# Two-block transformer stack on one core: the attention's score parts issued ahead of the rounds of transposes

## The chip, the cores and the metric

The kernel runs on one core of a Trainium2 chip, as one launch. The metric is the device time of a whole execution in microseconds (us), and the number compared is the median over runs. In this text PE is TensorE (matmuls and transposes), DVE is VectorE, ACT is ScalarE, POOL is GpSimd and SP is SyncE. Each engine works through its own queue in order, and engines wait for each other through semaphores.

## What is computed

Two blocks of two layers each, over 512 latent tokens and 256 context tokens of width 1024, in float32. Every layer is an attention mixer followed by a gated feed-forward net with a short convolution. The change touches only the attention of the first three layers. There the reference is, cut to the core:

```python
def diff_attn(q, k, v, lam):          # layers 0 and 1: 4 heads, 2 maps each
    s = jnp.einsum("bqhmd,bkhmd->bhmqk", q, k) * (B_QK_DIM ** -0.5)
    p = jax.nn.softmax(s, axis=-1)
    a = p[:, :, 0] - lam * p[:, :, 1]
    return jnp.einsum("bhqk,bkhd->bqhd", a, v)

# layer 2: 8 heads of dense attention, 8 heads of attention to a
# neighbourhood (a bias masks the rest), heads taken in pairs
s = jnp.einsum('bgrqd,bgkd->bgrqk', q, k) * scale   # + bias
p = jax.nn.softmax(s, axis=-1)
o = jnp.einsum('bgrqk,bgkd->bgrqd', p, v)
```

Latent queries attend to 768 keys (512 latent, 256 context), context queries to the 256 context keys.

## The kernel before

**Steps.** `Attention` (with `paired_groups`) cuts the attention of a layer into groups and steps. A group is one head (layers 0 and 1) or one pair of heads (layer 2). A step is 128 queries of a group and always has two sides, e = 0 and e = 1: the two maps of a head, or the two heads of a pair. I call a step LAT0 to LAT3 for the four latent query tiles (768 keys) and CTX0, CTX1 for the two context tiles (256 keys). Layer 0 has 4 groups of six steps, layer 1 has 4 groups of LAT0 to LAT3 only, and layer 2 has 8 groups of six: four "plain" ones and then four "near" ones, whose latent steps carry the bias.

**What happens to a step n.** PE multiplies the scores of both sides into PSUM (`scores`, in parts of 512 and 256 keys for a latent step: S0 and S1 below; one part for a context step). DVE takes the row maxima (`maxima`, L1986; in a near step L1977 to L1983), ACT the exponentials (`exps`, L1465; near L1461 and L1462), DVE the reciprocals of the row sums (`reciprocals`, L1946 or L1948), POOL multiplies the probabilities by them (L693), and in layers 0 and 1 DVE subtracts the second map (`difference`, L1959). Some steps later PE transposes the probabilities in rounds of three or four 128x128 blocks (`turn`, L1013: rounds T0, T1, T2) into a single PSUM half bank, `TURNS`, and ACT (L1446) or DVE (L1925) copies each round out to `PTR`. Last, PE multiplies by the values (`values`, called V below).

**Software pipeline.** In step n PE issues the scores of step n and the transposes of step n - lag, where lag is 3 in layers 0 and 1 and 2 in layer 2. A latent step of layers 0 and 1 has two rounds, a latent step of layer 2 three (four blocks each; T1 holds the last two of side 0 and the first two of side 1), and a context step one round. In layers 0 and 1 ACT copies all rounds. In layer 2 DVE copies T0 and ACT copies T1 and T2.

**Queues.** There is no scheduler: each engine's order is the order of its own Python loop over n. What matters here:
- PE, before: T0, S0, T1, S1, V, T2, V.
- ACT: the output copy (if one is due), the copies of the rounds, and then the exponentials of step n.
- DVE: in layer 2 the copy of T0, then the low half of an output (L1934, after ACT's L1434) if one is due, then the reciprocals of step n-1, then the maxima of step n; in layers 0 and 1 the difference of step n-1 ends the list.
- POOL: the two multiplications (one in layers 0 and 1) of each step, once the reciprocals are there.

**Waits.** The scores lie in three PSUM banks that rotate over the sides. So the first part of side 0 waits until the exponentials of step n-2 are done, and the first part of side 1 until side 0 of step n-1 is:

```python
for e, (qt, kt, rows) in enumerate(G["maps"]):
    if a == 0 and A.side(n, e) >= 3:
        pe.wait_ge(S.exp_done, A.side(n, e) - 2)
```

A round of transposes waits for its probabilities (`p_ready`) and for the copy of the round before (`pt_ready` for ACT's copies, `pt_dve` for DVE's). DVE may begin the maxima when the last score part is done (`s_done`).

Of the kernel before, what the change touches and what calls it, by code (L numbers as in the profile page):

```python
# [101 lines left out]
def build(nc, d, out):  # L102
# [55 lines left out]
    with ctx:  # L158
# [420 lines left out]
        def scores_psum(A, n, e):  # L579

            return PS[(2 * n + e) % 3]
# [200 lines left out]
        def _(pe):  # L782
# [4 lines left out]
            def mm(o, a, b, start, stop):  # L787
                return pe.matmul(o, a, b, start=start, stop=stop)  # L788
# [86 lines left out]
            def rs_read():  # L875

                if w.taken.get(S.rs_free, 0):
                    pe.wait_ge(S.rs_free, w.taken[S.rs_free])
# [122 lines left out]
            def attention(A):  # L1001
                base = A.base

                def turn(r, n):

                    p_at = A.p_base + (n + 1 if A.diff else 2 * n + max(e for e, _ in r["chunks"]) + 1)
                    pe.wait_ge(S.p_ready, p_at)
                    if r["act0"]:
                        pe.wait_ge(S.pt_ready, r["act0"])
                    if r["dve0"]:  # L1010
                        pe.wait_ge(S.pt_dve, r["dve0"])
                    for k, (e, j) in enumerate(r["chunks"]):
                        last = pe.transpose(TURNS[:, k * P:(k + 1) * P], A.slot(n, e)[1][:, j * P:(j + 1) * P], IDENT)  # L1013
                    last.then_inc(S.t_done, 1)

                def scores(n, a, m, last):

                    G, u = A.steps[n]
# [3 lines that stand above are left out]
                        k0 = G["j0"] * P + a  # L1022
                        at = G["q0"] + u * P
                        step = mm(scores_psum(A, n, e)[:, a:a + m], qt[rows, at:at + P], kt[rows, k0:k0 + m], True, True)
                        if last:
                            step.then_inc(S.s_done, 1)

                def values(it):

                    G, u, j = it["G"], it["u"], it["j"]  # L1030
                    if j == 0:
                        act_n, dve_n = A.copied[it["step"]]
                        pe.wait_ge(S.pt_ready, act_n)
                        if dve_n:
                            pe.wait_ge(S.pt_dve, dve_n)
                    if it["opens"] and outs[0]:
                        pe.wait_ge(S.o_free, outs[0])
                    if it["opens"]:
                        outs[0] += 1
                    at, c0 = 256 * (it["half"] % 2), P * (u - 1)  # L1040
                    for e, rows in enumerate(G["rows"]):
                        last = mm(OUTS[rows, c0:c0 + 256], G["v"][e](G["j0"] + j), PTR[:, NTC * e + j, at:at + 256],
                                  j == 0, j == G["nj"] - 1)
                    if j == G["nj"] - 1:
                        last.then_inc(S.v_done, 1)

                rs_read()
                for n in range(A.n):
                    turns, items = A.turns(n), list(A.items[n])
                    parts = []  # L1050
                    if n < len(A.steps):
                        nk = A.steps[n][0]["nj"] * P
                        parts = [(a, min(512, nk - a)) for a in range(0, nk, 512)]
                    for k in range(max(len(turns), len(parts))):
                        if k < len(turns):
                            turn(turns[k], n - A.lag)
                        if k < len(parts):
                            scores(n, *parts[k], k == len(parts) - 1)
                        if k and items:
                            values(items.pop(0))  # L1060
                    for it in items:
                        values(it)
                act_n, dve_n = A.copied[-1]
                pe.wait_ge(S.exp_done, A.side(len(A.steps), 0))
                pe.wait_ge(S.pt_ready, act_n)
                if dve_n:
                    pe.wait_ge(S.pt_dve, dve_n)
                pe.wait_ge(S.o_free, base["outs"] + len(A.groups))
                w.taken[S.exp_done] = A.side(len(A.steps), 0)
                w.taken[S.pt_ready] = act_n  # L1070
                w.taken[S.o_free] = outs[0]
                w.taken[S.p_ready] = A.p_base + len(A.steps) * (1 if A.diff else 2)
# [14 lines left out]
            for li, L in enumerate(layers):  # L1087
# [42 lines left out]
                if blk == 0:  # L1130
# [24 lines left out]
                    rope(range(4, 12))  # L1155
                    pe.wait_ge(S.qk_ready, w.seen(S.qk_ready))
                    attention(L["attention"])
                    norm([(c,) for c in range(4, 8)], T, False, big)
                elif l == 0:
# [6 lines left out]
                    pe.wait_ge(S.qk_ready, w.seen(S.qk_ready))  # L1166
                    pe.wait_ge(S.swap_landed, 32)
                    attention(L["attention"])
                else:
                    linear(L["w_in"], HH, HL, None, S.h_ready)  # L1170
# [1268 lines left out]
```

## Time and profile before

| | us |
|---|---|
| runs shown, median (lowest to highest) | 4388.65 (4376.14 to 4388.95) |
| the profiled execution: device time | 4390.87 |
| its span | 4389.3 |
| attention of layer 0, 403.79 to 511 | 107.2 |
| attention of layer 1, 1530 to 1620 | 90.0 |
| attention of layer 2, 2342.89 to 2585 | 242.1 |

| share of the stretch in which the engine is busy | PE | DVE | ACT | POOL | granted clock |
|---|---|---|---|---|---|
| whole span | 89% | 44% | 28% | 8% | 0.91 |
| layer 0 attention | 89% | 59% | 53% | 40% | 0.81 |
| layer 1 attention | 89% | 58% | 52% | 39% | 0.82 |
| layer 2 attention | 85% | 54% | 54% | 72% | 0.95 |

The granted clock is TensorE's, as a share of full speed. The modelled end of a matmul includes its pipeline, and waits inside a group of merged rows count as busy, so the PE share reads high. Outside the three stretches nothing of the attention loop runs.

### The profile page before, as it was taken

To read this page: it belongs to the slowest core of one execution; us is meant where nothing else is said; L and a number is where in the kernel's file an instruction comes from. 1 tells how busy PE (TensorE), PEld (TensorE's weight loads), DVE (VectorE), ACT (ScalarE), POOL (GpSimd) and SP (SyncE) were. 2 spreads that over 40 slices of the span, in tenths; PEclk is the share of its full clock that TensorE was granted. 3 is DMA by queue.
4 is the path that set the end of the run, shared out by engine and by line. 5 is a ranking of instruction groups with operands and counts; after the bars stand their busy time and mean duration, and the time that the engine had idled before them with its cause. 6 is when DMAs were issued, how large, how long until landed. Compare 5 with 4: busy or idle time off the path is not lost.

```text
span 4389.3 us, 50022 instructions
## 1 busy us (share of the span) xinstructions
PE 3890.7 (89%) x20239; PEld 2987.2 (68%) x20239; DVE 1945.1 (44%) x2991; ACT 1236.5 (28%) x1931; POOL 344.1 (8%) x323
## 2 busy tenths in 40 slices
PE   6977889999989788999898886999996799978997
PEld 4865668888868556777784465888885445556775
DVE  3444554324355355434314546433435344445454
ACT  3222422112122142222223542211212344433221
POOL 1030300000000030000004740000000000000000
PEclk8976889999999579999998998999998789899998
DMA  4530013333322003545220101333321000012331
GB/s 169 156 84 1 1 58 111 96 92 113 89 63 72 1 1 102 156 137 160 72 58 13 26 28 51 116 95 93 115 82 38 23 16 16 23 49 68 91 96 63
DMA packets 500133, 317.33 MB, mean 72 GB/s; under 512 B 26832, under 2 KB 492526, under 8 KB 499904
## 3 DMA queue, kind: packets, MB, share of 16 engines
q1 hardware_dynamic: 492144, 299.80, 23.2%
q0 software_dynamic: 7760, 14.32, 1.2%
q8 instruction: 162, 2.65, 0.3%
q14 instruction: 67, 0.55, 0.0%
HBM read 309.61 MB, written 4.55 MB: 72 GB/s over the span
## 4 chain that ended last, share of the span: by engine, by line
PE 78%; DVE 12%; ACT 4%; issue 3%; POOL 2%; DMA 0%; DVEq 0%; ACTq 0%; POOLq 0%
PE PS L788 75%; PE PS L1013 1%; DVE TMP L1805 1%; POOL TMP L693 1%; DVE TMP L2380 1%; ACT SPH L1276 1%; DVE SPL L1724 1%; DVE HL L1788 1%; DVE TMP L1741 1%; PE PS L971 1%; DVE TMP L1797 1%; DVE X L1748 1%; DVE ATT L1986 1%; POOL BIG L693 1%; DVE X L2341 1%
## 5 line engine op out<-in xcount | busy, mean ns | idle before, releaser
L788 PE MATMUL PS<-HH,SPH 128*128 128x512 f32 (+1 forms) x3424 | 1240.7, 362 | 115.6 <-DVE HL L1788 69.1
L788 PE MATMUL PS<-HL,SPH 128*128 128x512 f32 (+1 forms) x3424 | 1217.2, 356 | 0.0
L788 PE MATMUL PS<-HH,SPL 128*128 128x512 f32 (+1 forms) x3424 | 1216.6, 355 | 0.0
L788 PEld LDWEIGHTS PS<-HH,SPH 128*128 128x128 f32 x3424 | 656.1, 192 | 258.7 <-issue 132.4
L788 PEld LDWEIGHTS PS<-HH,SPL 128*128 128x128 f32 x3424 | 655.3, 191 | 93.1
L788 PEld LDWEIGHTS PS<-HL,SPH 128*128 128x128 f32 x3424 | 657.2, 192 | 87.9
L1724 DVE TENSOR_TENSOR SPL<-RAW,SPH 128x1024 fp32r<-128x1024 f32 (+3 forms) x371 | 459.3, 1238 | 550.5 <-ACT SPH L1276 550.4
L1276 ACT ACTIVATE SPH<-RAW 128x1024 fp32r<-128x1024 f32 (+3 forms) x371 | 393.6, 1061 | 590.7 <-PE PS L788 483.0
L788 PE MATMUL PS<-MH,SPH 128*128 128x512 f32 (+1 forms) x1056 | 379.4, 359 | 18.1 <-DVE ML L2393 18.1
L788 PE MATMUL PS<-ML,SPH 128*128 128x512 f32 (+1 forms) x1056 | 377.3, 357 | 0.0
L788 PE MATMUL PS<-MH,SPL 128*128 128x512 f32 (+1 forms) x1056 | 377.2, 357 | 0.0
L2034 DVE SCALAR_TENSOR_TENSOR X<-PS,MOD,X 128x512 f32<-128x512 f32 (+1 forms) x144 | 95.3, 662 | 534.1 <-PE PS L788 532.3
L1681 ACT ACTIVATE TMP<-TMP 128x768 f32<-128x768 f32 (+1 forms) x88 | 65.0, 739 | 688.8 <-DVE TMP L2380 688.8
L788 PEld LDWEIGHTS PS<-MH,SPH 128*128 128x128 f32 x1056 | 202.0, 191 | 50.2 <-DVE ML L2393 21.8
L2371 DVE TENSOR_SCALAR TMP<-PS,PCOL 128x768 f32<-128x768 f32 (+1 forms) x88 | 83.0, 943 | 313.7 <-PE PS L788 303.7
L788 PEld LDWEIGHTS PS<-ML,SPH 128*128 128x128 f32 x1056 | 202.3, 192 | 28.3
L788 PEld LDWEIGHTS PS<-MH,SPL 128*128 128x128 f32 x1056 | 201.8, 191 | 28.7
L788 PE MATMUL PS<-BIG 64*128 64x256 f32 (+1 forms) x528 | 168.8, 582 | 17.5 <-issue 6.5
L2380 DVE SCALAR_TENSOR_TENSOR TMP<-PS,PCOL,TMP 128x511 f32<-128x511 f32 (+1 forms) x264 | 174.5, 661 | 21.9 <-DVE TMP L2380 0.5
L1686 ACT ACTIVATE MH<-TMP 128x768 fp32r<-128x768 f32 (+1 forms) x88 | 65.0, 738 | 322.9 <-DVE TMP L2387 322.9
L788 PE MATMUL PS<-ONES,TMP 128*128 128x1 f32 x276 | 57.6, 336 | 97.8 <-DVE TMP L1741 72.8
L1986 DVE TENSOR_REDUCE ATT<-PS 128x1 f32<-128x768 f32 (+1 forms) x144 | 105.2, 772 | 71.1 <-PE PS L788 71.0
(297 smaller groups left out, 4166.8 us busy)
## 6 DMA issues: line engine op xcount, KB each, us to landing
MS<-in_l_w_ada SPq DMA_DIRECT2D x96, 512.0 KB, 3.7
RAW<-in_l_w_up SPq DMA_DIRECT2D x88, 512.0 KB, 4.7
MS<-in_w_mod SPq DMA_DIRECT2D x80, 512.0 KB, 3.7
RAW<-in_w_gate SPq DMA_DIRECT2D x44, 512.0 KB, 4.9
RAW<-in_w_val SPq DMA_DIRECT2D x44, 512.0 KB, 4.9
RAW<-in_w_down SPq DMA_DIRECT2D x32, 704.0 KB, 4.7
RAW<-in_l_w_down SPq DMA_DIRECT2D x32, 704.0 KB, 4.6
RAW<-in_w_in SPq DMA_DIRECT2D x40, 512.0 KB, 5.3
```

The costliest lines, as they stand in the source:

```text
L693: pool.tensor_scalar(ex[:, 0:nk], ex[:, 0:nk], ATT[:, 3, k:k + 1], None, ALU.mult)\
L788: return pe.matmul(o, a, b, start=start, stop=stop)
L971: last = pe.transpose(STAT[:, j * P:(j + 1) * P], src[:, j * P:(j + 1) * P], IDENT)
L1013: last = pe.transpose(TURNS[:, k * P:(k + 1) * P], A.slot(n, e)[1][:, j * P:(j + 1) * P], IDENT)
L1276: act.activation(SPH[slot][:, 0:kc, 0:m], RAW[slot][:, 0:kc, 0:m], ACT.Copy).then_inc(S.hi_ready, 1)
L1681: act.activation(TMP[0][:, 0:T], TMP[0][:, 0:T], ACT.Silu)\
L1686: act.activation(MH[:, f, 0:T], TMP[1][:, 0:T], ACT.Copy)\
L1724: dve.tensor_tensor(SPL[slot][:, 0:kc, 0:m], RAW[slot][:, 0:kc, 0:m], SPH[slot][:, 0:kc, 0:m].bitcast(F32), ALU.subtract).then_inc(S.lo_re ...
L1986: dve.tensor_reduce(ATT[:, 0, k:k + 1], ps[:, 0:nk], AX.X, ALU.max, negate=True)\
L2034: dve.scalar_tensor_tensor(out=xc, in0=LIN[s % 2][:, a:a + k], scalar=g, in1=xc, op0=ALU.mult, op1=ALU.add)\
L2371: dve.tensor_scalar(g[:, 0:T], ps[:, 0:T], tap(1), par(li, "fb", f + f0), ALU.mult, ALU.add)\
L2380: dve.scalar_tensor_tensor(out=g[:, a + da:a + da + m - 1], in0=ps[:, a + sa:a + sa + m - 1], scalar=tap(k), in1=g[:, a + da:a + da + m - ...
```

## The change

In PE's loop over the steps the two calls inside the loop over k change places. The score part k now goes ahead of the round of transposes k. The queues of DVE, ACT, POOL and SP are word for word the same, and no wait is added or taken out.

```diff
                     for k in range(max(len(turns), len(parts))):
+                        if k < len(parts):
+                            scores(n, *parts[k], k == len(parts) - 1)
                         if k < len(turns):
                             turn(turns[k], n - A.lag)
-                        if k < len(parts):
-                            scores(n, *parts[k], k == len(parts) - 1)
                         if k and items:
                             values(items.pop(0))
```

PE in layer 2, a latent step whose three rounds are due (LAT2 of the first plain group). L788 with BIG or TMP_69 on the right are the scores of the two sides, L1013 the transposes. Before:

```order
L1013 MATMUL PS<-CST,TMP_67 128x128 [waits pt_ready,p_ready]
L1013 MATMUL PS<-CST,TMP_67 128x128 x3
L788 MATMUL PS<-BIG 128x512 [waits exp_done]
L788 MATMUL PS<-TMP_69,BIG 128x512 [waits exp_done]
L1013 MATMUL PS<-CST,TMP_67 128x128 [waits pt_dve,pt_ready,p_ready]
L1013 MATMUL PS<-CST,TMP_67 128x128
L1013 MATMUL PS<-CST,TMP_68 128x128 x2
L788 MATMUL PS<-BIG 128x256
L788 MATMUL PS<-TMP_69,BIG 128x256
L1013 MATMUL PS<-CST,TMP_68 128x128 [waits pt_dve,pt_ready,p_ready]
```

and now:

```order
L788 MATMUL PS<-BIG 128x512 [waits exp_done]
L788 MATMUL PS<-TMP_69,BIG 128x512 [waits exp_done]
L1013 MATMUL PS<-CST,TMP_67 128x128 [waits pt_ready,p_ready]
L1013 MATMUL PS<-CST,TMP_67 128x128 x3
L788 MATMUL PS<-BIG 128x256
L788 MATMUL PS<-TMP_69,BIG 128x256
L1013 MATMUL PS<-CST,TMP_67 128x128 [waits pt_dve,pt_ready,p_ready]
L1013 MATMUL PS<-CST,TMP_67 128x128
L1013 MATMUL PS<-CST,TMP_68 128x128 x2
L1013 MATMUL PS<-CST,TMP_68 128x128 [waits pt_dve,pt_ready,p_ready]
```

T0 moved behind S0, and with it behind the wait for `exp_done`; T1 moved behind S1.

DVE in layer 2, three latent steps in a row (the same in both kernels). L1925 copies T0, L1934 writes an output's low half, L1946 is the reciprocals of the step before, L1986 the maxima:

```order
L1925 COPY PTR<-PS 128x4x128 [waits v_done,t_done]
L1934 TENSOR_TENSOR HL<-PS,HH 128x512 [waits o_hi]
L1946 RECIPROCAL ATT<-ATT 128x2 [waits exp_done]
L1986 TENSOR_REDUCE ATT<-PS 128x1 [waits s_done] x2
L1925 COPY PTR<-PS 128x4x128 [waits v_done,t_done]
L1934 TENSOR_TENSOR HL<-PS,HH 128x256 [waits o_hi]
L1946 RECIPROCAL ATT<-ATT 128x2 [waits exp_done]
L1986 TENSOR_REDUCE ATT<-PS 128x1 [waits s_done] x2
L1925 COPY PTR<-PS 128x4x128 [waits v_done,t_done]
```

Nothing moved here: the copy of T0 stands ahead of the reciprocals and the maxima.

PE in layer 1, a latent step with its two rounds (BIG alone under L788 are the scores of both sides, VT the values). Before:

```order
L1013 MATMUL PS<-CST,TMP_67 128x128 [waits pt_ready,p_ready]
L1013 MATMUL PS<-CST,TMP_67 128x128 x2
L788 MATMUL PS<-BIG 128x512 [waits exp_done] x2
L1013 MATMUL PS<-CST,TMP_67 128x128 [waits pt_ready,p_ready]
L1013 MATMUL PS<-CST,TMP_67 128x128 x2
L788 MATMUL PS<-BIG 128x256 x2
L788 MATMUL PS<-PTR,VT 128x256 [waits pt_ready]
```

and now:

```order
L788 MATMUL PS<-BIG 128x512 [waits exp_done] x2
L1013 MATMUL PS<-CST,TMP_67 128x128 [waits pt_ready,p_ready]
L1013 MATMUL PS<-CST,TMP_67 128x128 x2
L788 MATMUL PS<-BIG 128x256 x2
L1013 MATMUL PS<-CST,TMP_67 128x128 [waits pt_ready,p_ready]
L1013 MATMUL PS<-CST,TMP_67 128x128 x2
L788 MATMUL PS<-PTR,VT 128x256 [waits pt_ready]
```

The last score part moved ahead of T1, whose wait for ACT's copy of T0 it no longer stands behind; T0 moved in between the two parts.

## Rows read from the trace of the kernel before

**Rows 1.** Timeline, layer 1: start us, us, engine line op out<-in xcount [idle before <-releaser].

```profile
1555.28 1.82 DVE L1986 TENSOR_REDUCE ATT<-PS 128x1 f32<-128x768 f32 x2 [2.81 <-PE PS L788]
...
1561.47 1.82 DVE L1986 TENSOR_REDUCE ATT<-PS 128x1 f32<-128x768 f32 x2 [2.81 <-PE PS L788]
...
1600.76 0.90 ACT L1465 ACTIVATE BIG<-PS,ATT 128x768 f32<-128x768 f32 x1 [1.19 <-DVE ATT L1986]
...
1601.43 1.50 PE L788 MATMUL PS<-BIG 64*128 64x512 f32 x4
...
1603.16 0.52 PE L1013 MATMUL PS<-CST,BIG 128*128 128x128 f32 x3 [0.23 <-ACT PTR L1446]
1603.61 0.70 PE L788 MATMUL PS<-BIG 64*128 64x256 f32 x4
...
1604.34 1.82 DVE L1986 TENSOR_REDUCE ATT<-PS 128x1 f32<-128x768 f32 x2 [1.26 <-PE PS L788]
1605.39 0.90 ACT L1465 ACTIVATE BIG<-PS,ATT 128x768 f32<-128x768 f32 x1 [1.19 <-DVE ATT L1986]
...
1608.97 1.82 DVE L1986 TENSOR_REDUCE ATT<-PS 128x1 f32<-128x768 f32 x2 [1.26 <-PE PS L788]
```

**Rows 2.** Timeline, layer 0: the maxima of LAT0 to LAT3 and the next LAT0.

```profile
435.70 1.82 DVE L1986 TENSOR_REDUCE ATT<-PS 128x1 f32<-128x768 f32 x2 [3.48 <-PE PS L788]
438.99 1.81 DVE L1986 TENSOR_REDUCE ATT<-PS 128x1 f32<-128x768 f32 x2
442.59 1.82 DVE L1986 TENSOR_REDUCE ATT<-PS 128x1 f32<-128x768 f32 x2
447.70 1.82 DVE L1986 TENSOR_REDUCE ATT<-PS 128x1 f32<-128x768 f32 x2 [1.64 <-PE PS L788]
...
459.87 1.82 DVE L1986 TENSOR_REDUCE ATT<-PS 128x1 f32<-128x768 f32 x2 [3.20 <-PE PS L788]
```

**Rows 3.** Timeline, layer 2, ACT: side 0's exponentials of one plain group, LAT0 to LAT0.

```profile
2401.26 0.90 ACT L1465 ACTIVATE TMP<-PS,ATT 128x768 f32<-128x768 f32 x1 [2.63 <-DVE ATT L1986]
...
2404.78 0.90 ACT L1465 ACTIVATE BIG<-PS,ATT 128x768 f32<-128x768 f32 x1 [1.65 <-DVE ATT L1986]
...
2410.85 0.89 ACT L1465 ACTIVATE EXH<-PS,ATT 128x768 f32<-128x768 f32 x1
...
2415.55 0.89 ACT L1465 ACTIVATE TMP<-PS,ATT 128x768 f32<-128x768 f32 x1
...
2420.66 0.47 ACT L1465 ACTIVATE BIG<-PS,ATT 128x256 f32<-128x256 f32 x1
...
2425.19 0.47 ACT L1465 ACTIVATE EXH<-PS,ATT 128x256 f32<-128x256 f32 x1
...
2428.84 0.90 ACT L1465 ACTIVATE TMP<-PS,ATT 128x768 f32<-128x768 f32 x1 [2.63 <-DVE ATT L1986]
```

**Rows 4.** Timeline, the same group: side 1's scores in LAT1, rounds and copy in CTX1.

```profile
2402.30 0.69 PE L788 MATMUL PS<-BIG 64*128 64x512 f32 x1
...
2402.83 0.59 PE L788 MATMUL PS<-BIG 64*128 64x512 f32 x1
...
2421.08 0.66 PE L1013 MATMUL PS<-CST,TMP 128*128 128x128 f32 x4
...
2421.77 0.69 DVE L1925 COPY PTR<-PS 128x512 f32<-128x512 f32 x1 [3.50 <-PE PS L1013]
...
2422.38 0.16 DVE L1946 RECIPROCAL ATT<-ATT 128x2 f32<-128x2 f32 x1
...
2422.61 0.63 PE L1013 MATMUL PS<-CST,TMP 128*128 128x128 f32 x4 [0.24 <-DVE PTR L1925]
```

**Rows 5.** Timeline, a near group: LAT0's first exponentials, now and next; a weight load.

```profile
2489.09 0.72 ACT L1461 ACTIVATE TMP<-TMP,ATT 128x512 f32<-128x512 f32 x1 [3.12 <-DVE ATT L1983]
...
2490.41 0.30 PEld L788 LDWEIGHTS PS<-BIG 64*128 64x128 f32 x4 [0.64 <-ACT TMP L1462]
...
2519.09 0.72 ACT L1461 ACTIVATE TMP<-TMP,ATT 128x512 f32<-128x512 f32 x1 [3.12 <-DVE ATT L1983]
```

## The prediction

> **What bounds the kernel now.** I read the page first, to see that the attention of three layers is 107 + 90 + 242 = 439 us of 4389, and that nothing else can move, since the change touches one loop. Then I read the timeline of one repeating stretch of each kind and asked what each wait ended on. The reader is to see a different loop in each.
>
> In layer 1 a warm latent step takes 4.63 us, from one exponential (1600.76) to the next (1605.39) [rows 1]. The scores of side 1 start at 1601.86 (the four score rows end at 1602.93, and one side takes 0.38 + 0.69), 1.10 after that exponential. T1 then waits for ACT, which copies T0 only after both exponentials (idle 0.23 <- ACT PTR). S1 stands behind T1 at 1603.61, the maxima wait for S1 (idle 1.26), and 1.05 after them comes the next exponential. So the loop is ACT, T1, S1, maxima, ACT.
>
> In layer 2 a plain group takes 27.58 us from exponential to exponential of LAT0, in steps of 3.52, 6.07, 4.70, 5.11, 4.53 and 3.65 [rows 3]. There T0 is early: it waits for nothing of step n-1, and so DVE's copy of it, the reciprocals behind that copy, and T1 with ACT's copies are early too. A near group takes 30.00 us [rows 5].
>
> **The change, part by part.** No work is added or removed. What changes is what T0 and S1 stand behind.
>
> *Layer 1: S1 no longer stands behind T1.* New loop at the warm clock: exponential to side 1's scores 1.10; its two passes, up to T0, 1.00 (0.38 + 0.69, less the 0.07 by which a following group starts inside the modelled end, my estimate); T0 0.45 (as T1 to S1, 1603.16 to 1603.61); S1 to maxima 0.73; maxima to exponential 1.05. Sum 4.33, against 4.63: a gain of 0.30 [rows 1]. T1 and its copy now run beside the maxima: T1 starts 1.18 after T0 at the latest, and ACT is free for the exponential at 2.12 after T0, against 2.23 by the maxima. So next late is still the maxima, with 0.1 us to spare. From 1561.47 to 1608.97 there are ten such steps, 47.50 us in all [rows 1]: eight of 4.63 and two of about 5.1, where ACT copies an output ahead of T0's copy. That copy no longer counts, and these two gain 0.78. **Layer 1: 8 x 0.30 + 2 x 0.78 = 4.0 us faster.** The steps ahead of 1561.47 run at half the clock and 6.19 us each [rows 1]; there T1 sits directly behind S0 without waiting for ACT, T0 takes its place and nothing changes.
>
> *Layer 0: the same, but T0 is added to steps in which it was free.* LAT1 and LAT2 transpose a context step there: one round, T0, which ran while PE waited for the exponential anyway. These steps take 3.29 and 3.60 us, and their maxima wait for nothing of PE [rows 2]. Now T0 (two blocks, 0.31) stands between S0 and S1: 1.05 + 1.10 + 1.00 + 0.31 + 0.73 = 4.19, so +0.90 and +0.59. LAT3 (5.11 [rows 2]) has two rounds and falls to 4.33, -0.78. The entry to the next LAT0 (447.70 to 459.87 is three steps) gains about 0.5, because S1 leaves T1 behind, and loses about 1.1, because T0 of CTX0 and CTX1 and the values behind it come later. That is +0.6 by my reading, and between -0.5 and +1.5. Sum per group +1.3, and it occurs three times (the first group has no transposes in its first steps). **Layer 0: 4 us slower.**
>
> *Layer 2: T0 is put behind the exponential, and with it DVE's queue.* This is the large term. Side 1 of S0 waits for side 0 of step n-1's exponential. Before, T0 was issued ahead of that wait. Now T0 follows it, and behind T0 stand in this order DVE's copy of T0, then T1 (one PSUM half holds a round), ACT's copies of T1 and T2, and only then, in ACT's queue, the exponential of step n. That closes a loop from exponential to exponential:
> - exponential to side 1's scores 1.04 (2401.26 [rows 3] to 2402.30 [rows 4]);
> - their two passes 1.08 (2402.30 to 2402.83 + 0.59, less the same small overlap) [rows 4];
> - T0 to DVE's copy 0.69, the copy 0.69, copy to T1 0.15 [rows 4];
> - T1 to the exponential 2.58 (2422.61 [rows 4] to 2425.19 [rows 3]): copy of T1, T2, copy of T2.
>
> Sum 6.23 for a latent step. LAT2 and LAT3 took 6.07 and 4.70 [rows 3], so +0.16 and +1.53. CTX0 has only 256 keys to score (about 0.65 in place of 1.08): 5.80 against 5.11, +0.69. CTX1 waits for a short exponential (about 0.5 in place of 1.04): 5.26 against 4.53, +0.73. LAT1 has one round and no copies on ACT. Its path is 1.04 + 1.08 + 0.69 + 0.69, then the reciprocals about 0.15 and maxima to exponential 1.05, together 4.70 against 3.52, +1.18: the maxima stand behind the copy too. LAT0 has its scores ahead of T0 now, and the copy, the reciprocals and the maxima follow: about +0.4. **Per plain group +4.7 us.** In a near group side 0's exponential takes 1.32 to release PE (2489.09 to 2490.41 [rows 5]) and maxima to exponential about 1.45. The same sum gives 5.5 + 6.5 + 6.5 + 6.1 + 5.3 + 4.5 = 34.4 against 30.00, **+4.4**. POOL's multiplications start later by as much as the reciprocals do, but they are not the last to arrive: their results are wanted two steps later.
>
> Against this stands that S1 no longer waits behind T1 for POOL and the copy. The maxima of LAT2 could start about 1 us earlier. It brings nothing, since ACT reaches the exponential by way of T2's copy, later than the maxima.
>
> Four groups at 4.7 and four at 4.4 are 36.4. The first group has nothing to transpose in its first two steps (-1.2) and the last has no next LAT0 (-0.4). **Layer 2: 34.8 us slower.**
>
> Sum: 34.8 + 4 - 4.0 = 34.8. On the profiled execution's 4390.87 that is 4425.7. This execution lies 2.2 above the median of the runs, so 4423.5, and I say 4424.
>
> One rule of the Trainium skill speaks against my main term. "TensorE: Matmul & The Clock Gate" (section "Architectural detail") says that PE's queue can pull weight loads ahead of matmuls in flight. If T0 could slip past the waiting scores, its cost would vanish. The row here speaks otherwise: side 1's own weight load stood still until the exponential was done (idle 0.64 <- ACT [rows 5]), so nothing behind a waiting instruction had been loaded. With the rule layer 2 would be unchanged and the sum 4389.
>
> **The rivals.**
> *A, the forecast (0.60):* the loop through T0 costs 3 to 5.5 us per group of layer 2. 4424, between 4410 and 4434.
> *B, the clock falls as well (0.17):* longer waits of PE in layer 2 send it to half clock in stretches. At half clock a latent step of layer 1 took 6.19 in place of 4.63, 1.56 more [rows 1]. One or two such steps in each of eight groups are 12 to 25 us on top: 4436 to 4449. The same page (Part 1) has it that activity releases a default throttle, which would allow this. For it: layer 1 ran its first steps at half clock. Against it: PE stays busy some 80% of each new group.
> *C, slack (0.14):* my sum takes every link as if nothing ran beside it. If the copies or T2 come in half a step earlier (POOL or the values were what held them), layer 2 loses only 1 or 2 us per group: +8 to +16, less 4: 4393 to 4401, within 0.3%.
> *D, faster (0.09):* the effect of layer 1 holds everywhere. If the maxima, not ACT's copies, close layer 2's loop, S1's freedom from T1 gives back what the maxima idled in LAT2 and CTX1, about 1 us in each of 2 steps of 8 groups: -16, and -4 of layer 1, and layer 0 even: 4369. It decides for D if DVE can take the maxima before T0's copy is in. By the queue's order it can't, so I give this little.
> That the change does nothing is the middle of C: PE's order does change in about every step.
>
> **How the numbers follow.** I take 0.3% (13 us) as what a measurement of this kernel can tell from no change. Slower by more (over 4402): A, B and a little of C, 0.81. Within: the rest of C and a little of A and D, 0.13. Faster by more (under 4375): 0.06. The range of 4400 to 4448 takes in A with its bounds, nearly all of B and the top of C, and leaves out some 2 in 10.
>
> **What would show it.** In layer 2 the copy L1925 comes later and its idle time before it grows; the reciprocals L1946 start right behind the copy, about 4.5 us after the maxima of the step before; the group grows from 27.6 to about 32.3 and from 30.0 to about 34.4; transposes no longer wait for POOL but for exponentials and copies. In layer 1 a warm step falls from 4.63 to 4.33, with S1 right behind T0. In layer 0 LAT1 grows by 0.9. I am wrong if layer 2's copies do not stand behind the scores in time, or if the exponentials of LAT3 still follow at 4.7 us. A lower granted clock in layer 2 would point to B.

## The result and the profile after

The changed kernel takes **4447.62 us** (median, 4444.85 to 4451.15) beside 4382.40 for the kernel before on the same chip (4369.07 to 4388.95): a ratio of **1.0153, 95% interval 1.0124 to 1.0182**. It is slower, as forecast, but by 65 us where the forecast said 35. Its ratio on the median that the forecast started from (4388.65) gives 4455.8, and that is 8 us beyond the range of 4400 to 4448; the median itself lies 0.4 us inside its upper end. The four runs of the kernel before were on the low side here: in the three later rounds its median was 4384.5 to 4391.1, and the two profiled executions are 55 us apart.

The profiled execution has a span of 4444.7 us (before 4389.3) and a granted clock of 0.906 (before 0.911). I measure each attention stretch from the start of its first row maximum to the start of ACT's last output copy, in one profile of each kernel:

| us | before | after | change | forecast |
|---|---|---|---|---|
| layer 0 | 106.38 | 119.83 | +13.45 | +4 |
| layer 1 | 90.13 | 86.92 | -3.2 | -4.0 |
| layer 2 | 241.46 | 294.40 | +52.9 | +34.8 |

The three come to +63. The span grew by 55, since the stretches between them, in which every instruction is the same, vary from one profile to another by some microseconds, and in one place by up to 14 (see runs 4 and 9).

*Layer 1*, the timeline after (start us, us, engine line op out<-in xcount, idle before and its releaser), one step at full clock ("warm" below), which answers to [rows 1]:

```profile
1602.10 0.90 ACT L1465 ACTIVATE TMP<-PS,ATT 128x768 f32<-128x768 f32 x1
...
1602.80 1.47 PE L788 MATMUL PS<-BIG 64*128 64x512 f32 x4
...
1604.20 0.55 PE L1013 MATMUL PS<-CST,BIG 128*128 128x128 f32 x3
...
1604.68 0.70 PE L788 MATMUL PS<-BIG 64*128 64x256 f32 x4
...
1605.41 1.82 DVE L1986 TENSOR_REDUCE ATT<-PS 128x1 f32<-128x768 f32 x2 [0.99 <-PE PS L788]
...
1606.46 0.90 ACT L1465 ACTIVATE BIG<-PS,ATT 128x768 f32<-128x768 f32 x1
```

S1 (1604.68) follows T0 at once and waits for no copy. The step is 4.36 us, 4.63 before; the sum said 4.33.

*Layer 0*, the maxima of LAT0 to LAT3 and the next LAT0, which answer to [rows 2]:

```profile
436.61 1.82 DVE L1986 TENSOR_REDUCE ATT<-PS 128x1 f32<-128x768 f32 x2 [3.47 <-PE PS L788]
440.86 1.82 DVE L1986 TENSOR_REDUCE ATT<-PS 128x1 f32<-128x768 f32 x2 [0.88 <-PE PS L788]
445.11 1.82 DVE L1986 TENSOR_REDUCE ATT<-PS 128x1 f32<-128x768 f32 x2 [0.88 <-PE PS L788]
449.48 1.82 DVE L1986 TENSOR_REDUCE ATT<-PS 128x1 f32<-128x768 f32 x2 [0.99 <-PE PS L788]
...
463.70 1.82 DVE L1986 TENSOR_REDUCE ATT<-PS 128x1 f32<-128x768 f32 x2 [3.69 <-PE PS L788]
```

The maxima of LAT1 and LAT2 now wait 0.88 for PE; in [rows 2] they waited for nothing of it. The three steps are 4.25, 4.25 and 4.37 (the sum said 4.19, 4.19, 4.33). The way on to the next LAT0 is 14.22 against 12.17, where I had +0.6.

*Layer 2*, side 0's exponentials of one plain group on ACT, LAT0 to LAT0, which answer to [rows 3]:

```profile
2389.84 0.90 ACT L1465 ACTIVATE TMP<-PS,ATT 128x768 f32<-128x768 f32 x1 [3.12 <-DVE ATT L1986]
2394.40 0.90 ACT L1465 ACTIVATE BIG<-PS,ATT 128x768 f32<-128x768 f32 x1 [2.69 <-DVE ATT L1986]
...
2400.61 0.90 ACT L1465 ACTIVATE EXH<-PS,ATT 128x768 f32<-128x768 f32 x1
...
2406.82 0.90 ACT L1465 ACTIVATE TMP<-PS,ATT 128x768 f32<-128x768 f32 x1
...
2414.71 0.47 ACT L1465 ACTIVATE BIG<-PS,ATT 128x256 f32<-128x256 f32 x1
...
2420.14 0.47 ACT L1465 ACTIVATE EXH<-PS,ATT 128x256 f32<-128x256 f32 x1
...
2424.28 0.90 ACT L1465 ACTIVATE TMP<-PS,ATT 128x768 f32<-128x768 f32 x1 [3.12 <-DVE ATT L1986]
```

The steps are 4.56, 6.21, 6.21, 7.89, 5.43 and 4.14, the forecast 4.70, 6.23, 6.23, 5.80, 5.26 and about 4.0: five of six within 0.2, and CTX0 off by 2.1. The group takes 34.44 (27.58 before); a near group, which answers to [rows 5], takes 36.55 (30.00). The rounds of LAT3 in that group, which answer to [rows 4]:

```profile
2401.65 1.12 PE L788 MATMUL PS<-TMP,BIG 64*128 64x512 f32 x2
...
2402.70 0.66 PE L1013 MATMUL PS<-CST,BIG 128*128 128x128 f32 x4
...
2403.40 0.69 DVE L1925 COPY PTR<-PS 128x512 f32<-128x512 f32 x1 [3.13 <-PE PS L1013]
...
2404.24 0.41 PE L1013 MATMUL PS<-CST,BIG 128*128 128x128 f32 x2 [0.24 <-DVE PTR L1925]
...
2404.34 0.15 DVE L1946 RECIPROCAL ATT<-ATT 128x2 f32<-128x2 f32 x1
...
2404.58 4.38 POOL L693 TENSOR_SCALAR EXH<-EXH,ATT 128x768 f32<-128x768 f32 x2 [1.55 <-DVE ATT L1946]
```

Scores, T0, copy, T1: each stands directly behind the one before it, the loop of the forecast. Link by link it is 1.04 from the exponential (2400.61) to side 1's scores, 1.05 for their passes, 0.70 to the copy, 0.84 to T1 and 2.58 to the next exponential (2406.82). The groups by line say the same for the whole run: ahead of ACT's copies L1446 the engine idled, until a transpose came,

```profile
  PE PS L1013: 184.2, 130
```

us and times, against 107.8 and 102 before; ahead of DVE's copy L1925 it was 160.5 against 67.2.

Where CTX0's 2.1 us are is in the windows of the kernel after (length, busy time and instructions of each engine, PEclk, DMA share, GB/s): the LAT1 and LAT2 steps, LAT3, the 6.9 us after it, and the rest of the group:

```profile
2389.84:2400.61 10.77, 10.35 (x57) 4.67 (x53) 6.39 (x11) 5.38 (x12) 7.32 (x5) 1.00 0.00 0
2400.61:2407.80 7.19, 5.27 (x24) 2.42 (x22) 2.81 (x5) 4.28 (x12) 5.64 (x4) 1.00 0.00 0
2407.80:2414.70 6.90, 5.97 (x22) 3.35 (x24) 1.41 (x4) 2.03 (x6) 4.86 (x3) 0.51 0.00 0
2414.70:2424.28 9.58, 8.49 (x60) 4.46 (x56) 3.19 (x9) 3.19 (x13) 3.38 (x4) 1.00 0.01 2
```

PE was busy 5.27 of the 7.19 us of LAT3 and the start of CTX0, and then ran at half clock (0.51, that is 1.2 GHz) through CTX0. The last of its idle time is the wait of side 1's scores in CTX0 for an exponential:

```profile
2407.86 1.22 PE L788 MATMUL PS<-TMP,BIG 64*128 64x256 f32 x2 [0.94 <-ACT TMP L1465]
```

A stretch of half clock comes once in each group behind the first, and the first runs at half clock for most of its length. Before, a whole plain group ran at 1.00:

```profile
2401.26:2428.84 27.58, 24.13 (x156) 13.22 (x152) 14.61 (x29) 14.87 (x39) 21.15 (x13) 1.00 0.00 1
```

### The profile page after: what moved, and what is told of

Its sections match the earlier page's. It is cut to its first block, busy times and chain, and to the rows that moved or that the text cites. A ratio compares the mean times of both kernels' runs of the same rounds, so it can differ in the third digit from the quotient of the medians.

```text
span 4444.7 us, 50022 instructions
## 1 busy us (share of the span) xinstructions
PE 3936.0 (89%) x20239; PEld 2994.2 (67%) x20239; DVE 1941.2 (44%) x2991; ACT 1238.9 (28%) x1931; POOL 344.5 (8%) x323
## 4 chain that ended last, share of the span: by engine, by line
PE 81%; DVE 12%; ACT 4%; issue 3%; POOL 0%; DMA 0%; DVEq 0%; SPq 0%; ACTq 0%; POOLq 0%
PE PS L788 76%; PE PS L1013 3%; DVE TMP L1805 1%; DVE TMP L2380 1%; ACT SPH L1276 1%; DVE HL L1788 1%; DVE SPL L1724 1%; DVE TMP L1741 1%; PE PS L971 1%; DVE TMP L1797 1%; DVE PTR L1925 1%; DVE X L1748 1%; DVE X L2341 1%; DVE TMP L2371 0%; DVE X L2344 0%
## 5 line engine op out<-in xcount | busy, mean ns | idle before, releaser
L788 PE MATMUL PS<-HH,SPH 128*128 128x512 f32 (+1 forms) x3424 | 1240.7, 362 | 116.5 <-DVE HL L1788 69.8
L788 PE MATMUL PS<-HL,SPH 128*128 128x512 f32 (+1 forms) x3424 | 1216.7, 355 | 0.0
L788 PE MATMUL PS<-HH,SPL 128*128 128x512 f32 (+1 forms) x3424 | 1216.4, 355 | 0.0
L788 PEld LDWEIGHTS PS<-HH,SPH 128*128 128x128 f32 x3424 | 656.3, 192 | 259.2 <-issue 132.5
L788 PEld LDWEIGHTS PS<-HH,SPL 128*128 128x128 f32 x3424 | 655.2, 191 | 93.0
L788 PEld LDWEIGHTS PS<-HL,SPH 128*128 128x128 f32 x3424 | 657.2, 192 | 87.8
L788 PE MATMUL PS<-MH,SPH 128*128 128x512 f32 (+1 forms) x1056 | 379.1, 359 | 18.1 <-DVE ML L2393 18.1
L788 PE MATMUL PS<-ML,SPH 128*128 128x512 f32 (+1 forms) x1056 | 377.6, 358 | 0.0
L788 PE MATMUL PS<-MH,SPL 128*128 128x512 f32 (+1 forms) x1056 | 377.1, 357 | 0.0
L788 PEld LDWEIGHTS PS<-MH,SPH 128*128 128x128 f32 x1056 | 201.9, 191 | 50.5 <-DVE ML L2393 21.8
L788 PE MATMUL PS<-BIG 64*128 64x256 f32 (+1 forms) x528 | 195.8, 607 | 32.9 <-issue 6.5
L788 PEld LDWEIGHTS PS<-MH,SPL 128*128 128x128 f32 x1056 | 201.8, 191 | 28.7
L788 PEld LDWEIGHTS PS<-ML,SPH 128*128 128x128 f32 x1056 | 202.0, 191 | 28.2
L788 PEld LDWEIGHTS PS<-BIG 64*128 64x128 f32 x528 | 71.0, 217 | 108.7 <-issue 42.0
L788 PE MATMUL PS<-ONES,TMP 128*128 128x1 f32 x276 | 55.8, 330 | 97.8 <-DVE TMP L1741 72.8
```

## The experiments

Three questions. Which of the two moves (T0 behind S0, S1 ahead of T1) costs what? Is the path of layer 2 really the one through DVE's copy of T0? And what does the clock cost beside it? All twelve were timed in rounds beside the kernel before, and each ratio is to the runs of its own round; the table gives the attention stretches of one profile of each, as above.

| us | total | ratio to before (95%) | layer 0 | layer 1 | layer 2 |
|---|---|---|---|---|---|
| before | 4382 to 4391 | 1 | 106.4 | 90.1 | 241.5 |
| after | 4447.62 | 1.0153 (1.0124 to 1.0182) | 119.8 | 86.9 | 294.4 |
| 1 change in layer 2 only | 4442.96 | 1.0112 (1.0088 to 1.0136) | 106.4 | 90.1 | 294.5 |
| 2 change in layers 0, 1 only | 4392.62 | 0.9997 (0.9984 to 1.0011) | 119.9 | 86.9 | 241.5 |
| 3 only T0 and S0 swapped | 4469.59 | 1.0189 (1.0166 to 1.0212) | 129.6 | 101.3 | 296.3 |
| 4 only T1 and S1 swapped | 4345.00 | 0.9899 (0.9884 to 0.9914) | 96.7 | 73.5 | 242.3 |
| 5 T0 between the sides of S0 | 4399.33 | 1.0026 (1.0003 to 1.0050) | 107.5 | 91.1 | 267.4 |
| 6 fillers in all steps of layer 2 | 4448.62 | 1.0159 (1.0122 to 1.0195) | 119.8 | 88.1 | 305.3 |
| 7 reciprocals ahead of the copy | 4437.76 | 1.0140 (1.0103 to 1.0178) | 119.7 | 85.6 | 290.9 |
| 8 fillers in CTX0 of layer 2 | 4430.84 | 1.0101 (1.0067 to 1.0135) | 119.3 | 88.3 | 279.9 |
| 9 as 4, in layers 0, 1 only | 4338.69 | 0.9911 (0.9878 to 0.9944) | 96.3 | 73.5 | 241.7 |
| 10 one-round steps as before | 4429.33 | 1.0101 (1.0068 to 1.0133) | 109.2 | 86.9 | 280.7 |
| 11 as 4, and 7 | 4370.50 | 0.9976 (0.9957 to 0.9994) | 96.6 | 73.5 | 263.2 |
| 12 fillers in CTX0 of layer 0 | 4444.13 | 1.0147 (1.0118 to 1.0176) | 116.6 | 88.1 | 292.2 |

### Where the loss is: one layer at a time (1, 2)

The first keeps the old order in layers 0 and 1 (below, against the changed kernel), the second in layer 2 (the same with `A.diff` in place of `not A.diff`):

```diff
-                        if k < len(parts):
+                        if not A.diff and k < len(parts):
                             scores(n, *parts[k], k == len(parts) - 1)
                         if k < len(turns):
                             turn(turns[k], n - A.lag)
+                        if not (not A.diff) and k < len(parts):
+                            scores(n, *parts[k], k == len(parts) - 1)
```

> The change in layer 2 only; layers 0 and 1 as before. Theory 1 (the loop through T0 and DVE's copy, plus PE at half clock in part of each group): the attention of layer 2 goes from 241 to 294 us, so +53 us in all, the plain group 34.4 us with 6.2 us for LAT2 and LAT3. Theory 2 (the loss was made in layers 0 and 1, or comes from the clock that these leave behind): under +25 us.

> The change in layers 0 and 1 only; layer 2 as before. Theory 1: layer 0 +13 us, layer 1 -3 us, so +10 us, and layer 2 at 241 us. Theory 2: +30 us or more.

In these two runs each layer keeps its own change to 0.1 us whatever the others do. Over all runs equal code repeats less well: with the changed order untouched, layer 1 took 86.9 to 88.3 us (runs 6, 8, 10 and 12) and layer 2 took 292.2 in run 12 for 294.4. A difference of some 2 us between two stretches therefore shows little by itself. Layer 2 alone costs 53 us of stretch and 52 of median. Layers 0 and 1 have +13.5 and -3.2 in their stretches, yet the median of the second did not move: the unchanged stretch behind layer 0 was 1010 us long in its profile and 1020 before. So I compare stretches below, and medians only where they differ by more than such shifts.

### Which of the two moves: (3, 4, 9)

```diff
-                        if k < len(parts):
+                        if k == 0 and k < len(parts):
                             scores(n, *parts[k], k == len(parts) - 1)
                         if k < len(turns):
                             turn(turns[k], n - A.lag)
+                        if not (k == 0) and k < len(parts):
+                            scores(n, *parts[k], k == len(parts) - 1)
```

This is run 3. Run 4 has `k > 0` in place of `k == 0`, and run 9 `A.diff and k > 0`. Run 3 gives S0, T0, T1, S1 and run 4 gives T0, S0, S1, T1; the change is both.

> Only T0 and S0 change places (S0, T0, T1, S1, V, T2), in all three layers. Theory 1: T0 is behind the exponential as in the change, so layer 2 is about as slow, +50 to +60 us. Layer 1 has T0, ACT's copy, T1 and then S1 in its loop, 5.5 us a step at the full clock in place of 4.6: +9 us, where the whole change had -3. In all +70 to +90 us. The rival that S1's early place costs something itself (the copies and T1 pushed back by it): layer 2 clearly under +50 us.

> Only T1 and S1 change places (T0, S0, S1, T1, V, T2), in all three layers. Theory 1: T0 stays ahead of the wait for the exponential, so nothing of the loss is left; the maxima come earlier. Layer 1: -3 to -5 us; layer 2: 0 to -8 us; layer 0: -2 to -5 us. In all -5 to -18 us. The rival that S1's place costs: slower than before.

> T1 and S1 change places in layers 0 and 1 only (T0, S0, S1, T1); layer 2 as before. Since layer 2 gained only 0.4 us a group from it, this should be within 5 us of the run that had it in all three layers, 35 to 50 us under before: layer 0 at 97 us, layer 1 at 73 us. Rival (half or more of that gain came from layer 2 or from what followed it): under 25 us gained.

The two moves have opposite signs. Run 3 came out as expected: +79 us in all, +55 in layer 2, and 5.55 us for a warm step of layer 1. Putting T0 behind S0 costs 52 us in layer 2 (294.4 against 242.3 of run 4), 23 in layer 0 and 13 in layer 1. Putting S1 ahead of T1 gains 9.7 us in layer 0 and 16.7 in layer 1 and nothing in layer 2 as a whole. There its plain groups at full clock fell by 0.4 us each (27.2 for 27.6), but the first group ran longer at half clock (33.1 us for 29.7), and the near groups too had half clock. So the change carried a good half and a bad half, and my 4.0 us in layer 1 was the net of both. I had expected a gain of 5 to 18 us of run 4, and it is 46: the sign was right, the size was not. DVE's maxima in layer 1 of run 4 (the two lines of edit shift L1986 to L1988):

```profile
1559.47 1.82 DVE L1988 TENSOR_REDUCE ATT<-PS 128x1 f32<-128x768 f32 x2 [0.22 <-PE PS L788]
...
1563.48 1.82 DVE L1988 TENSOR_REDUCE ATT<-PS 128x1 f32<-128x768 f32 x2 [0.41 <-PE PS L788]
...
1567.07 1.82 DVE L1988 TENSOR_REDUCE ATT<-PS 128x1 f32<-128x768 f32 x2 [0.22 <-PE PS L788]
```

A warm step is 3.6 to 4.0 us there, against 4.63 before and 4.36 after: T0 runs in PE's wait for the exponential, and S1 waits for nothing. Run 4 also left half clock early. Its latent steps of layer 1 are warm from the fifth on, 15 us after the first maximum; before, half clock lasted 30 us of that layer. The attention stretches account for 25.5 of the 44.4 us by which the spans of the two profiles differ. The rest is in unchanged stretches at another granted clock, here the one from layer 0's end to layer 1's start, before and then in run 4:

```profile
513.13:1533.37 1020.24, 932.46 (x5241) 781.99 (x5242) 431.90 (x602) 217.48 (x270) 16.39 (x32) 0.91 0.26 75
```

```profile
501.66:1508.14 1006.48, 917.82 (x5241) 769.23 (x5242) 431.78 (x602) 217.46 (x270) 16.39 (x32) 0.93 0.26 76
```

Why the same 5241 matmuls get 0.93 in one profile and 0.91 in another isn't settled, and the order ahead of them alone doesn't decide it. With the order of before in layer 0 this stretch was 1020 us in one profile and 1013 in another (run 1), and with the changed order 1017, 1010 (run 2) and 1007 (run 8). In the three profiles with only T1 and S1 changed places it was 1006 each time. Run 9 confirms the place: with layer 2 left as it was, it is 0.9911, the same gain within the intervals. Runs 4 and 9 beat both kernels; of their 46 us each the attention stretches account for 25.5 and 26.5.

### Is it the path through T0's copy: (5, 7, 11)

Run 5 issues T0 right after side 0's part, ahead of side 1's wait for the exponential:

```diff
-                def scores(n, a, m, last):
+                def scores(n, a, m, last, between=None):
...
+                        if e == 0 and between is not None:
+                            turn(between, n - A.lag)
```

> The change, but T0 is issued between the two sides of the first score part, so behind side 0's scores and ahead of side 1's wait for the exponential (order: S0 of side 0, T0, S0 of side 1, S1, T1, V, T2). Theory 1 (what costs is that T0 stands behind the wait for the exponential): nothing of the loss is left and S1 is still ahead of T1, so about as fast as with only T1 and S1 changed, 30 to 50 us under before. Rival (what costs is T0's later place as such, some 0.9 us of scores ahead of it): half of the loss or more stays, +25 us or more.

It gave back half of layer 2's loss (267.4, still 25.9 over before), so my first theory fails there and the rival's +25 us or more holds for that layer, though the median is only 8 over. Both parts of the loss shrank: the plain groups stayed at full clock (1.00) and took 30.4 us, where the changed order takes 32.3 at full clock (run 8 below) and the kernel before 27.6. Here a second effect showed, in PE's timeline of run 5 (scores 64 rows deep):

```profile
2390.32 1.12 PE L788 MATMUL PS<-BIG 64*128 64x512 f32 x2
2391.38 0.66 PE L1013 MATMUL PS<-CST,BIG 128*128 128x128 f32 x4
2391.96 0.69 PE L788 MATMUL PS<-TMP,BIG 64*128 64x512 f32 x1
...
2393.45 0.44 PE L1013 MATMUL PS<-CST,BIG 128*128 128x128 f32 x2
```

and in that of the kernel before, where the sides follow each other (the rows of side 1 that lie between and behind these two are in [rows 4]):

```profile
2402.14 0.69 PE L788 MATMUL PS<-TMP,BIG 64*128 64x512 f32 x1
...
2402.67 0.59 PE L788 MATMUL PS<-TMP,BIG 64*128 64x512 f32 x1
```

Side by side both sides are done 1.28 us after the first starts (2402.14 to 2402.83 + 0.59). Held apart, a side takes 1.12 by itself: side 0 here, and both sides in the changed kernel, where side 1 waits for its exponential (2401.65 above). And T1 starts 2.07 us behind T0 (2391.38 to 2393.45), since side 1's scores and S1 lie between, where in the changed kernel it is 1.54 (2402.70 to 2404.24). So run 5 moves more than T0's wait, and doesn't say cleanly how much of the loss that wait was.

Runs 7 and 11 move DVE's reciprocals ahead of its copy of T0, in the changed kernel and in run 4:

```diff
+                    if 1 <= n <= len(A.steps):
+                        reciprocals(n - 1)
...
-                    if 1 <= n <= len(A.steps):
-                        reciprocals(n - 1)
```

> The change, with DVE's reciprocals of step n-1 ahead of its copy of T0 in all layers. Theory 1 (the loop closes through T0, DVE's copy, T1, ACT's copies and the exponential; POOL's multiplications are not the last to arrive): POOL starts some 1.5 us earlier and nothing is gained, 0 to -4 us against the change. Rival (the late reciprocals and POOL are the loop): most of the +53 us of layer 2 comes back, -30 us or more against the change.

> T1 and S1 change places in all three layers (T0, S0, S1, T1), and DVE's reciprocals of step n-1 stand ahead of its copy of T0. POOL is near its bound in the latent steps of layer 2 there (4.4 us of work in steps of 4.7 to 5.8), so its earlier start should show: layer 2 from 242 to 230-240 us, 2 to 12 us under the run with the pair changed alone, 47 to 57 us under before. Rival: POOL starts earlier only where it then waits anyway; the same as that run within 3 us.

In the changed kernel the copy is late anyway, and the earlier reciprocals (and POOL behind them) bring at most 3.5 us: POOL's lateness is not what costs 53. In run 4 the copy was early, and the reciprocals, which wait for the exponentials of step n-1, push it late again. Layer 2 went from 242.3 to 263.2, against my expectation, which had DVE free to wait there. The timeline of run 11 shows the wait in a LAT3 (T0, reciprocals, copy, T1):

```profile
2400.01 0.63 PE L1013 MATMUL PS<-CST,BIG 128*128 128x128 f32 x4 [0.15 <-issue]
...
2401.70 0.17 DVE L1948 RECIPROCAL ATT<-ATT 128x2 f32<-128x2 f32 x1 [2.41 <-ACT EXH L1467]
2401.78 0.69 DVE L1927 COPY PTR<-PS 128x512 f32<-128x512 f32 x1
...
2402.62 0.41 PE L1013 MATMUL PS<-CST,BIG 128*128 128x128 f32 x2 [0.22 <-DVE PTR L1927]
```

The copy starts 1.77 us after T0, in run 4 0.66 (T0 at 2393.74, copy at 2394.40), and T1 now waits for it. PE's queue is that of run 4. This order of DVE costs 21 us, with half-clock stretches back (0.50 in 2375.5 to 2382.3, and once in each group from there to the last): a plain group is 28.2 us at full clock and 29.7 to 30.3 with half clock, where run 4 had 27.2, and the near groups are 34.2 for 29.8 to 31.7. So a late copy of T0 is enough for a good part of the loss, though T0 itself is early.

### The clock, apart from the loop: (6, 8, 12)

Each adds matmuls between the two sides of the scores, into columns that nothing reads. Run 8:

```diff
                     for e, (qt, kt, rows) in enumerate(G["maps"]):
...
+                        if e == 0 and not A.diff and n >= 2 and G["q0"] and u == 0:
+                            ps = scores_psum(A, n, 0)
+                            for _ in range(2):
+                                mm(ps[:, 768:1024], IDENT, kt[:, 0:256], True, True)
```

Run 12 has `A.diff` in place of `not A.diff`. Run 6 puts one of 128 or 256 columns in every step of layer 2 from the third on, and two in CTX0.

> The change, with extra matmuls in layer 2 whose results nobody reads, into unused columns of the score bank between side 0 and side 1 of the first part, where PE waits for the exponential: two of 256 columns in CTX0, one in the other steps (128 columns wide in the latent steps of the plain groups). Theory 1 with half clock as a part of its own: PE is busier, the clock stays at its full level, CTX0 goes from 7.9 to about 6 us and the plain group from 34.4 to about 32.4; layer 2 from 294 to 276-284 us, so 10 to 18 us less than the change. Rival (the 2 us are no matter of the clock but of the order in CTX0): the fillers only add, 294 us or more.

> The change, with two extra matmuls of 256 columns (results unread) in CTX0 of layer 2 alone, between side 0 and side 1 of the scores. In the run with fillers in every step the clock held and CTX0 took 5.83 us, but the other steps paid for their fillers. Theory: with the filler only where PE idles, the full clock holds through CTX0 (7.9 to 5.9 us) and nothing else changes, 8 groups x 2 us: layer 2 from 294 to 276-282 us, 12 to 18 us less than the change. Rival: without the other fillers the clock falls all the same, or falls elsewhere; layer 2 at 290 us or more.

> The changed kernel with added work in layer 0: two matmuls of 256 columns that nothing reads, between the two sides of CTX0's scores in each of the four heads (eight matmuls in all). Read is layer 0, which took 119.83 us in the changed kernel and 106.38 before. Theory 1 (half clock is part of the loss between CTX1 and the next LAT0, 7.4 us in place of 5.4, and at the end): the fillers keep TensorE at full clock through CTX0 as they did in layer 2, the half-clock stretch of 6.8 us per head goes or is much shorter, and layer 0 falls by 4 to 12 us, to 108 to 116. Theory 2 (the loss there is T0, its copy and the values coming later, and the half clock follows from the waiting without costing much): the fillers cost what they last, 0 to 0.9 us per head, and layer 0 is 119.5 to 123. Layers 1 and 2 stay at 87 and 294. The total moves by no more than 12 us.

Run 6 held full clock too and gave CTX0 its 5.83 us, but in the other steps its fillers stood on the loop and cost more than they gave (group 36.28). Run 8 has them only where the half clock had been. Side 0's exponentials on ACT:

```profile
2382.48 0.90 ACT L1469 ACTIVATE TMP<-PS,ATT 128x768 f32<-128x768 f32 x1 [3.12 <-DVE ATT L1990]
...
2399.46 0.89 ACT L1469 ACTIVATE TMP<-PS,ATT 128x768 f32<-128x768 f32 x1
...
2405.29 0.47 ACT L1469 ACTIVATE BIG<-PS,ATT 128x256 f32<-128x256 f32 x1
...
2414.77 0.90 ACT L1469 ACTIVATE TMP<-PS,ATT 128x768 f32<-128x768 f32 x1 [3.12 <-DVE ATT L1990]
```

and its windows over LAT1 to LAT3 and over CTX0:

```profile
2382.48:2399.46 16.98, 15.53 (x78) 7.09 (x74) 9.20 (x16) 8.68 (x20) 11.96 (x8) 1.00 0.00 0
2399.46:2405.29 5.83, 4.74 (x29) 2.89 (x30) 1.42 (x4) 3.02 (x9) 4.72 (x3) 1.00 0.01 3
```

With more work on PE the group takes **32.29 us, where the sum of the forecast said 32.3**, and CTX0 5.83, where it said 5.80. The near groups but the last take 34.35, where it said 34.4. Layer 2 is 14.5 us shorter: 15.2 in the seven groups behind the first, less 0.7 in the first, which has its half clock still. So the half clock of the repeating groups was some 15 us of the changed kernel's layer 2 (the kernel before had some 4 us of its own, in the first and the last near group). LAT3 is the same with the fillers as without, 5.17 us of PE in 6.21; what is gone is the wait of 0.94 us for the exponential in CTX0, which came on top of it. By Part 1 of the Trainium skill's "TensorE: Matmul & The Clock Gate" activity releases the throttle, and these rows agree: 1.00 with the fillers, 0.51 without. In layer 0 (run 12) the half-clock stretch of the second head fell from 6.8 to 3.4 us, that of the third is gone, and the layer fell by 3.3: from CTX1's maxima to the next LAT0's it is now 6.73 and 5.09 us, where it was 7.44 and 7.45. That is just outside the range of the first theory (108 to 116) and far from the second's, so the clock has a share of the loss there, and a smaller one than I had put it at. The sum alone would be weak, since layer 2, which this run leaves as it was, moved by 2.2 us too. The third head says it better: 27.10 us in the changed kernel, 25.13 at full clock, 24.03 before.

### The steps with one round: (10)

```diff
-                        if k < len(parts):
+                        if len(turns) != 1 and k < len(parts):
                             scores(n, *parts[k], k == len(parts) - 1)
                         if k < len(turns):
                             turn(turns[k], n - A.lag)
+                        if not (len(turns) != 1) and k < len(parts):
+                            scores(n, *parts[k], k == len(parts) - 1)
```

> The change, except that steps with one round of transposes keep the order of before (T0, S0, S1): LAT1 and LAT2 of layer 0, LAT0 and LAT1 of layer 2. Theory 1: layer 0's LAT1 and LAT2 fall from 4.25 to 3.3 and 3.6 us, three times, layer 0 from 120 to 113-116 us; layer 2's LAT1 falls from 4.56 to about 3.5 us, 8 groups, 294 to 283-287 us. The steps with three rounds stay at 6.2 us. In all 12 to 18 us less than the change. Rival (these steps only wait for what the others delay): no more than 4 us less.

Steps with one round have the old order here. It brought 10.7 us in layer 0 and 13.7 in layer 2, more than the 4 to 7 and 7 to 11 that I expected, and layer 1, which has no such steps, is unchanged. LAT1 of a plain group is 3.52 again, where it was 4.56; the forecast had charged it 1.18. In layer 0 LAT1 and LAT2 are as short together as before (6.88 us a head, 6.89 before, 8.50 in the changed kernel), which is 4.9 of the 10.7. The rest came behind them: the way from CTX1 to the next LAT0 fell from 7.44 to 6.20 (5.38 before), with 3.4 us of half clock per head in place of 6.8, and the end of the layer by 2.8.

## Why the prediction was right and where it was wrong

*Right, and shown.* The sign. The loop of layer 2, link by link: 6.21 us where 6.23 was worked out (side 1's passes are 1.05; the forecast wrote 1.08, though its own row less its own overlap gives 1.05). The group, too, once the clock is held: the three plain groups behind the first take 14.1 us more in run 8 than before, and the forecast had 14.1; a near group takes 4.3 more, forecast 4.4; and the last group takes 38.5, against 34.5 in run 9, the profile in which the old order had full clock there, forecast +4.0. That DVE's copy of T0 stands in that loop: T1 waits for the copy in the rows after, and in run 11 a late copy alone brings part of the loss. Rival D wanted 2 us per group of layer 2 from S1's freedom from T1; at full clock it is 0.4 (run 4). Rival C's slack doesn't exist: the loop takes what its links add up to. Layer 1's step (4.36 for 4.33). Layer 0's LAT1 to LAT3 (+0.96, +0.65, -0.74 for +0.90, +0.59, -0.78). The rule of the Trainium skill on weight loads that are pulled ahead ("TensorE: Matmul & The Clock Gate", section "Architectural detail") did not help T0: it starts at 2402.70, behind side 1's scores of 2401.65, and not in the wait ahead of them. The rule speaks of weight loads only, and T0's matmuls would have had to pass the waiting scores as well, so the forecast gave it more than it says.

*The step that failed: A and B as rivals.* The forecast summed layer 2 at full clock, and gave a chance of 0.17 that "the clock falls as well". They are no alternatives. The loop adds waits of PE (1.04 us in LAT3 and 0.94 more as CTX0 starts), and the half clock came behind them in each of the steady groups, at 2.1 us a group. My argument against it, that PE stays busy for some 80% of a group, was an average, and it can't tell the kernels apart: PE is busy 87% of a plain group in both (24.13 of 27.58, 30.08 of 34.44). The rows to look at were those of LAT3 and CTX0, where the waits of PE come together. The price that I had for B was of the right size (12 to 25 us in all, and 18 were missing), but not of the right place: it stood for latent steps, and the half clock took CTX0 and the first group. That A + B, 4436 to 4449, holds the measured 4447.6 is in part luck, since layer 0 was 9 us over its forecast too. Layer 2 by groups, against the forecast:

| | change measured | forecast |
|---|---|---|
| first group | +11.0 | +3.5 |
| three plain groups | +6.9, +6.8, +6.7 | +4.7 each |
| three near groups | +4.4, +6.7, +7.7 | +4.4 each |
| last group | +2.8 | +4.0 |

In the first of the three near groups the kernel before had half clock itself (0.89, 32.2 us for 30.0), so its +4.4 hides 2.2 us; the same holds for the last group (0.91, 36.7 us, and 34.5 in run 9 at full clock). Seven and a half of the 18 us that were missing are in the first group alone. It begins at half clock in both kernels, and a latent step of the new loop takes 8.8 us at that clock (ACT's exponentials at 2354.53, 2363.31 and 2372.07) against 6.21. The old order had left half clock after about 12 us, the new one after about 32. I had priced that group at full clock too.

*Layer 0: a term mis-sized, and two left out.* Of the +13.45, the first head has +2.7, the second and third +2.9 and +3.1, and the last +4.8; the forecast had 0 and three times +1.3. In the middle heads the term that failed is the entry to the next LAT0: I put it at +0.6 (up to +1.5), and it is +2.1. It holds 6.8 us of half clock per head where before it held 3.4. Run 10 takes it apart. CTX0 and CTX1 have two rounds due in layer 0, so they keep the new order there, and with LAT1 and LAT2 alone put back the entry is +0.8, near the forecast's reason for it (T0 of CTX0 and CTX1 comes later). The other 1.3 came with the longer half clock behind the late LAT1 and LAT2. Run 12 points the same way: its third head, at full clock, is 1.1 us over before (which had its 3.4 us of half clock), where the forecast said 1.3. The first head, and the end behind the last CTX1 (14.35 us for 10.44, +3.9), I had at nothing of their own. Run 10 gives back 2.8 of that end and only 0.3 of the first head, and how these two divide between T0's place and the clock is open.

*Layer 1: right by a sum whose parts I hadn't seen.* I asked only what S1's freedom brings with T0 in its new place. Run 4 shows the same freedom to be worth 16.7 us with T0 left where it was, the shorter stretch at half clock included.

## What to carry to other kernels

Price the two halves of a swap one by one: here one gains 1% and the other loses 2%. Here a short round of transposes was free ahead of a wait, and behind it the whole chain that hangs on it joined the loop; so try putting transposes whose copies others need ahead of scores that wait for exponentials, and score parts that wait for nothing ahead of transposes that wait for a copy. And where a change adds waits to PE, sum the stretch at both clocks, and look for the place where PE's waits come together: the busy share of the group was 87% with the loss and without it.

## What the runs showed of the chip that I had not expected

- Matmuls of 64 rows on the two halves of the partitions ran beside each other where they were neighbours in PE's queue and were free to start close together: two sides of two passes of 512 columns ended 1.28 us after the first started (before). With a round of transposes between them (run 5), or with the second waiting for an exponential (after), a side took 1.12 by itself.
- More work made the kernel faster: eight pairs of unread 256-column matmuls (1.13 us a pair) took 14.5 us off layer 2, and from its second group on PE stayed at full clock (1.00).
- The same loop costs 6.21 us at full and 8.8 us at half clock. DVE's copy of T0 takes 0.69 at either. If PE's part doubles, it is 2.6 of the 6.21, and the links of DVE and ACT are the other 3.6 (an estimate from the two times).
- The granted clock of a long stretch behind the edited one differed between profiles with equal instructions (0.91 and 0.93 over some 1010 us, worth 14 us), also where the order ahead of it was the same (1020 and 1013 us, 1017 and 1007 us). Its cause stays open.
